# Stick-breaking attention, one core: the last pair of heads takes its query blocks in another order, and ScalarE's copies are reordered in every step

## The reference

```python
def block(args):                      # 128 queries, 16 heads of 64
    i, qi = args
    ...
    zlog = jnp.einsum('bqhd,bkhd->bhqk', qi, kp) * scale
    log_beta = jax.nn.log_sigmoid(zlog)
    log_keep = jnp.where(valid, log_beta - zlog, 0.0)
    after = lax.cumsum(log_keep, axis=3, reverse=True) - log_keep
    w = jnp.where(valid, jnp.exp(log_beta + after), 0.0)
    return jnp.einsum('bhqk,bkhd->bqhd', w, vp)
```

## Time and profile before

| | |
|---|---|
| median of 3 runs | 2334.75 us (2331.86 to 2334.78) |
| the profiled execution | 2333.68 us, its span 2331.9 us |
| TensorE busy in the span | 2202.1 us (94%) |
| VectorE busy | 1592.7 us (68%) |
| ScalarE busy | 1036.3 us (44%) |
| mean granted TensorE clock | 0.982 |

### The profile page before, as it was taken

How to read it: one execution, slowest core, us unless ns; L and a number is a source line. 1 busy time by engine, 2 the same in 40 slices (tenths; PEclk the granted TensorE clock), 3 DMA queues, 4 the chain that set the end, 5 groups by cost and what they waited for, 6 DMA issues and landing times. The chain is left out here.

```text
span 2331.9 us, 44629 instructions
## 1 busy us (share of the span) xinstructions
PE 2202.1 (94%) x18332; PEld 1411.5 (61%) x18332; DVE 1592.7 (68%) x2016; ACT 1036.3 (44%) x1883; POOL 607.0 (26%) x379
## 2 busy tenths in 40 slices
PE   7999998899999889989999999999999999999997
PEld 4666665555555556656666665458644445588846
DVE  7876887888888855787777774257688484236544
ACT  3226765667666643434444443235543232124221
POOL 3555762000000120064333331000256442001060
PEclk9999999999999989999999999999999999989998
DMA  3113213676766631211111113326333612032412
GB/s 130 48 52 101 82 55 71 116 130 125 135 126 126 110 107 63 94 41 50 55 55 59 55 51 118 101 74 212 124 102 104 212 55 82 23 101 72 158 60 73
DMA packets 279377, 216.24 MB, mean 93 GB/s; under 512 B 194752, under 2 KB 245120, under 8 KB 277776
## 3 DMA queue, kind: packets, MB, share of 16 engines
q1 hardware_dynamic: 279184, 213.51, 34.0%
HBM read 145.77 MB, written 25.76 MB: 74 GB/s over the span
## 5 line engine op out<-in xcount | busy, mean ns | idle before, releaser
L1519 DVE TENSOR_TENSOR_SCAN att_left<-att_left,att_unseen_prefix 16x16 f32<-16x16 f32 (+5 forms) x144 | 177.9, 1276 | 28.2 <-ACT att_left L1332 26.9
L2912 PE MATMUL ps<-second_x_hi,whi_z 128*128 128x512 f16 (+1 forms) x480 | 179.1, 373 | 2.6 <-DVE second_x_lo L1740 1.4
L1219 PE MATMUL ps<-x_hi,whi_z 128*128 128x348 f16 x560 | 176.7, 315 | 4.7 <-DVE att_q L1450 4.7
L2913 PE MATMUL ps<-second_x_lo,whi_z 128*128 128x512 f16 (+1 forms) x480 | 178.8, 372 | 0.0
L2914 PE MATMUL ps<-second_x_hi,wlo_z 128*128 128x512 f16 (+1 forms) x480 | 178.8, 372 | 0.0
L1221 PE MATMUL ps<-x_hi,wlo_z 128*128 128x348 f16 x560 | 175.3, 313 | 0.0
L1220 PE MATMUL ps<-x_lo,whi_z 128*128 128x348 f16 x560 | 175.3, 313 | 0.0
L1352 ACT ACTIVATE att_left_split<-att_left 128x256 f16<-128x256 f32 (+7 forms) x128 | 87.2, 681 | 111.9 <-DVE att_left L1519 111.1
L2215 PE MATMUL ps<-x_lo,whi_z 128*128 128x342 f16 x432 | 133.2, 308 | 0.0
L2214 PE MATMUL ps<-x_hi,whi_z 128*128 128x342 f16 x432 | 132.8, 308 | 0.0
L2216 PE MATMUL ps<-x_hi,wlo_z 128*128 128x342 f16 x432 | 132.6, 307 | 0.0
(11 more groups left out here) (657 smaller groups left out, 6438.7 us busy)
## 6 DMA issues: line engine op xcount, KB each, us to landing
wraw_z<-in_w_second SPq DMA_DIRECT2D x30, 512.0 KB, 3.6
wraw_z<-in_w_up SPq DMA_DIRECT2D x26, 512.0 KB, 3.5
wraw_z<-in_w_qkv SPq DMA_DIRECT2D x24, 512.0 KB, 4.2
wraw_z<-in_w_down SPq DMA_DIRECT2D x20, 512.0 KB, 4.3
raw_down<-in_w_down SPq DMA_DIRECT2D x20, 512.0 KB, 4.1
seg<-dt_a_sums SPq DMA_DIRECT2D x18, 512.0 KB, 5.1
wraw_z<-in_w_up SPq DMA_DIRECT2D x36, 256.0 KB, 3.7
second_work<-parked_units SPq DMA_DIRECT2D x7, 1280.0 KB, 6.0
```

The source lines that it names most:

```text
L1219: nc.tensor.matmul(lin_ps(g), hi, xhi, start=(kb == 0), stop=False)
L1519: nc.vector.tensor_tensor_scan(x, x, unseen, 1.0, ALU.mult, ALU.max).then_inc(s_scan, 1)
L2912: nc.tensor.matmul(out, hi, xhi, start=(j == 0), stop=False)
L2913: nc.tensor.matmul(out, hi, xlo, start=False, stop=False)
```

## The change

Three things change together. Pair 7 takes its blocks in the order 6, 7, 8, 3, 4, 5, 0, 1, 2; position in the pair is now `i`, and work that was bound to a pair's first steps (`v_steps`, `values_high`, `values_low`, `turn_v`, `copy_v`, `split_values`, the squares) goes by `i`, the lengths by `j`. The stash goes by `stash` (j = 3, or in pair 7 the first step), at the end of the two banks of each head. In every step ScalarE has `copy_w` and `split_high` ahead of `left_high(s, 1)` and `values_high`, and in the second step of a pair `copy_v` behind `left_high(s, 0)`. TensorE has `turn_v` in the middle of a projection and not ahead of it.

```diff
@@ -1020,10 +1020,26 @@
...
+LAST_ORDER = (6, 7, 8, 3, 4, 5, 0, 1, 2)
+SENDS = 2 * NSTEP - 1
+
+
+def sent_order(blocks):
+
+    counts = [2 * (j > 0) + (i == 0) for i, j in enumerate(blocks)]
+    return [sum(counts[:i]) for i in range(NSTEP)]
+
+
+SENT_OF = sent_order(range(NSTEP)), sent_order(LAST_ORDER)
+V_SENT = [SENDS * p + (2 if p == PAIRS - 1 else 0) for p in range(PAIRS)]
+
+
 class Step:
...
     def __init__(self, n):
-        self.n, self.p, self.j = n, n // NSTEP, n % NSTEP
+        self.n, self.p, self.i = n, n // NSTEP, n % NSTEP
+        self.j = self.i if self.p < PAIRS - 1 else LAST_ORDER[self.i]
+        self.stash = self.j == 3 if self.p < PAIRS - 1 else self.i == 0
         self.rows = P if self.j else META
@@ -1037,7 +1053,7 @@
...
-        return SENDS * self.p + 2 * self.j - 1 + a
+        return SENDS * self.p + SENT_OF[self.p == PAIRS - 1][self.i] + a
@@ -1055,7 +1071,6 @@
...
 PSCALE = 32768.0
-SENDS = 2 * NSTEP - 1
 SENT_SLOTS, SENT_SIGNALS = 3, 4
@@ -1106,7 +1121,7 @@
...
         z_ps = lambda a: flat[:, (2 + 2 * a) * BANK:(4 + 2 * a) * BANK]
-        z_more = flat[:, 2 * BANK:6 * BANK].rearrange("p (a n) -> p a n", a=2)[:, :, BANK:BANK + META]
+        z_more = flat[:, 2 * BANK:6 * BANK].rearrange("p (a n) -> p a n", a=2)[:, :, 2 * BANK - META:2 * BANK]
         turn_ps = S.ps[:, 6, :]
@@ -1147,7 +1162,7 @@
...
                 def turn_values(p):
-                    e = SENDS * p
+                    e = V_SENT[p]
                     sp.wait_ge(s_left_lo, e + 1)
@@ -1159,7 +1174,7 @@
...
                             turn_left(s, a)
-                    else:
+                    if ATT[s].i == 0:
                         turn_values(ATT[s].p)
@@ -1224,7 +1239,7 @@
...
                     t = ATT[n]
-                    if t.j == 0:
+                    if t.i == 0:
                         pe.wait_ge(s_low, 2 * NT * (t.p + 1))
@@ -1234,7 +1249,7 @@
...
                                                         start=(i == 0), stop=(i == 2))
-                    if t.j == 3:
+                    if t.stash:
                         for i, (x, y) in enumerate(PASSES):
@@ -1257,8 +1272,10 @@
...
                         pe.wait_ge(s_o, n)
-                    if t.j == 1:
-                        pe.wait_ge(*landed(SENDS * t.p))
+                    if t.i == 0:
+                        pe.wait_ge(s_vlo, t.p + 1)
+                    if t.i <= 1 and t.j:
+                        pe.wait_ge(*landed(V_SENT[t.p]))
                     if t.j:
@@ -1268,8 +1285,6 @@
...
                                                      skip_group_check=True)
-                    else:
-                        pe.wait_ge(s_vlo, t.p + 1)
                     pe.wait_ge(s_wlo, n + 1)
@@ -1285,10 +1300,12 @@
...
                         scores(s)
-                    if s < STEPS and ATT[s].j == 1:
+                    if s + GROUPS < (QKV_B + EARLY) * NT:
+                        linear(s + GROUPS, 0, DB // 2)
+                    if s < STEPS and ATT[s].i == 1:
                         turn_v(ATT[s].p)
                     if s + GROUPS < (QKV_B + EARLY) * NT:
-                        linear(s + GROUPS, 0, DB)
+                        linear(s + GROUPS, DB // 2, DB)
                     if 1 <= s <= STEPS:
@@ -1323,7 +1340,7 @@
...
                                 act.wait_ge(s_left_lo, ATT[n - 3].sent(1) + 1)
-                    if a == 1 and t.j == 3:
+                    if a == 1 and t.stash:
                         nc.scalar.activation(left_more[:, 0:META], z_more[:, 0, :], ACT.Sigmoid, scale=-0.125)
@@ -1417,27 +1434,26 @@
...
                             odds(s, a)
-                        if ATT[s].j == 1:
-                            copy_v(ATT[s].p)
                         if ATT[s].j:
                             left_high(s, 0)
+                        if ATT[s].i == 1:
+                            copy_v(ATT[s].p)
                     if s % NT == 0 and s // NT + BY_POOL < QKV_B + EARLY:
...
                         chunk_high(NORMED_AT[s - 1])
-                    if s < STEPS:
-                        if ATT[s].j:
-                            left_high(s, 1)
-                        else:
-                            values_high(ATT[s].p)
                     if 1 <= s <= STEPS:
...
                         split_high(s - 1)
+                    if s < STEPS and ATT[s].j:
+                        left_high(s, 1)
+                    if s < STEPS and ATT[s].i == 0:
+                        values_high(ATT[s].p)
                     if s >= LAG:
                         store(s - LAG)
-                    if s < STEPS and ATT[s].p and ATT[s].j == 4:
+                    if s < STEPS and ATT[s].p and ATT[s].i == 4:
                         square(ATT[s].p - 1)
@@ -1539,28 +1555,28 @@
...
                         continue
-                    if ATT[s].j == LAG:
+                    if ATT[s].i == LAG:
                         split_values(ATT[s].p)
...
                     scan(s, 1)
-                    if ATT[s].j == 0:
+                    if ATT[s].j:
+                        left_low(s, 0)
+                    if ATT[s].i == 0:
                         v_steps(ATT[s].p)
-                    else:
-                        left_low(s, 0)
                     if s + GROUPS in SPLIT:
...
                         left_low(s, 1)
-                    else:
+                    if ATT[s].i == 0:
                         values_low(ATT[s].p)
...
                     p = ATT[s].p - 1
-                    if p >= 1 and ATT[s].j == 5:
+                    if p >= 1 and ATT[s].i == 5:
                         add_square(p)
...
```

## The result

The changed kernel takes 2342.81 us (median of 7 runs, 2340.23 to 2345.68) against 2333.86 for the kernel before (7 runs, 2329.51 to 2334.78): ratio 1.0040, interval 1.0028 to 1.0052. It is slower, by 9 us where +1.5 was forecast. The profiled execution took 2341.88 us, 8.2 more than that of before.

What follows compares the result with a forecast made beforehand. TensorE was taken as the bound (94% busy), with VectorE close behind. Pair 7's order -7.4, copies +5.4 and clock +3.5 gave +1.5 us on the profiled 2333.7, so 2335.2, stated as 2336; range 2326 to 2344.

Steps and rivals of the forecast that it cites:

- the likeliest case: Whole kernel: shorter tail paid back by VectorE's lag and boundary waits; 2336 us, within 0.2%, chance 0.40.
- The copies, +1.1 a pair: Pairs 2 to 6: copies moved in every step make VectorE late; TensorE waits 1.3 and 2.5; +5.4 us in all.
- Two more stretches of half clock, +3.5: Pair boundaries: longer waits drop TensorE's clock to 1.2 GHz twice more, +3.5 us, between none and six (10.5).
- Rival B: Pair boundaries: the longer wait drops the clock at every one, 1.75 us each; all six give 2343 us; chance 0.31.
- Pair 7's order, -7.4: Pair 7 and tail: the new order shortens the tail by 12.6 us and costs 5.2 inside the pair.
- 3.0 was reckoned for the long values: Inside pair 7: 18 long value blocks move ahead out of the tail, about 0.17 us each at full clock.
- 2.2 was reckoned: Inside pair 7: new waits of 7.8 us against 5.6 of waits before, so +2.2 us.
- the forecast 7.8: Pair 7: two new TensorE waits, 2.7 us for v_steps before turn_v and 5.1 for copy_v.
- the 2.2 of the kernel before's "long blocks": Pair 7: 2.2 us of earlier waits in its long blocks, counted among the 5.6 set against the new waits.
- not 7.1: Tail: from the end of the last projection to the next phase 7.1 us, 12.6 less than 19.74.
- the 0 for pairs 0 and 1: Pairs 0 and 1: later low parts still end with GpSimd's work, so 0 us; shared bandwidth instead would cost 4.5 more.

Runs made afterwards that it cites:

- e3: The changed kernel with copy_v back ahead of left_high(s, 0): 2332.55 us, ratio 0.9997 to the kernel before.
- e7: The kernel before with copy_w and split_high ahead of left_high(s, 1) at j = 3 and 6 alone: 2349.47 us, ratio 1.0066 to the kernel before.
- e9: The changed kernel with GpSimd's two output-weight conversions on 16 of 1024 columns (wrong weights, timing only): 2336.39 us, ratio 1.0016 to the kernel before.
- e10: The changed kernel with copy_v ahead of left_high(s, 0), copy_w and split_high ahead only in a pair's first step and j = 7, 8: 2321.57 us, ratio 0.9950.
- e1: The changed kernel with pair 7 in natural order, the copies as changed: 2341.27 us, ratio 1.0033 to the kernel before.

## Where the prediction held and where it failed, point by point

The range held the time (2326 to 2344); the likeliest case and the centre missed it. That the range reached so far was in part luck: its upper end was put there for the clock falling at all six boundaries, which did not happen. By the prediction's own steps:

- **The copies, +1.1 a pair, nothing in pairs 0 and 1, 5.4 in all.** Right in size. Pair 3 pays 1.06. Pair 2 begins 0.06 earlier than before, so pairs 0 and 1 cost nothing in sum; but that is a net figure, as TensorE's idle time in them rose by 0.5 and its busy time fell by 0.6, with 3.4 us less at half clock in pair 0. The waits are 1.16 (forecast 1.3) and 2.38 (forecast 2.5). The copies alone are 7.9 slower, where this term and the next make 8.9. The prediction gave VectorE's lag as the cause and `copy_v` as the place where it shows; e3 has the same lag (1.17 before the meta product in pair 3, as the changed kernel has in pair 4) and pays nothing in pairs 2 to 6, so in this kernel the cost needs `copy_v`'s place as well.
- **Two more stretches of half clock, +3.5.** Right in size at the boundaries: pairs 2 and 5 have one each at about 1.6. Both terms together, 8.9, are what pair 7's start is late, 8.8. Rival B's drop at all six boundaries did not come: its time was reached in another way.
- **Pair 7's order, -7.4: the step that failed.** The profiles give 75.37 to 74.08, -1.3, and the missing 6.1 falls into three pieces. *TensorE's busy time inside the pair* rose by 5.8 (50.03 to 55.80), where 3.0 was reckoned for the long values. The rest is half clock inside pair 7: 6.8 us at 0.52 that begin inside the wait of 4.89, and 3.4 at 0.53 behind the wait of 2.38, some 4.3 us lost where the earlier trace rows's stretch lost 1.7, so 2.6 more. The clock term spoke of boundaries alone. *Its waits* rose by 4.4 (5.60 to 9.96), where 2.2 was reckoned. 2.56 and 4.89 are 7.45, the forecast 7.8. The prediction let the 2.2 of the kernel before's "long blocks" go; but 1.5 of those stood behind the same collision of GpSimd and VectorE, which with the new order falls on the j = 5 block again and costs 2.38 (the two rows of the kernel before below). *The tail* is 8.3 and not 7.1: its low part takes 1.98 in place of 0.40, which with the rest as reckoned would give 8.7. With short GpSimd work the tail is about 6.8 (822.8 to 829.57). 2.6 + 2.2 + 1.2 make 6.0 of the 6.1.

```profile
790.30 4.26 DVE L1478 SCALAR_TENSOR_TENSOR att_left_split<-att_left,att_left_split 128x640 f16<-128x640 f32 x2
```

```profile
796.91 0.23 PE L1274 MATMUL ps<-att_w_meta_split,att_v_meta_split 96*128 96x128 f16 x1 [1.51 <-DVE att_w_meta_split L1462]
```

- **The two parts do not add.** The order alone gained 3.7 us, the change lost 9.0. The prediction summed the terms as if the copies in pair 7 were free. In the tail they put VectorE's low part behind GpSimd's start: the tail is 8.3 with both, 6.4 with the order alone, and about 6.8 with both and short GpSimd work. Of the 4.3 us between the two pairs 7 that is 1.9; the other 2.4 lies for the most part in the steps of its second and third block (15.9 and 7.5 us against 14.3 and 6.5). It was not taken apart.
- **Outside the attention** 0.7 of the 8.2 remains: the stage begins 0.75 earlier in the profile after and what follows its end takes 1.4 longer, with the first 5.08 us of the next phase at 0.50. The prediction put this at nothing; in the other profiles what follows the end of the attention varies from 1500.8 to 1506.2 us (before: 1503.2), so no effect of the change is shown there.
- **VectorE beside GpSimd.** The reading of the earlier trace rows fits what followed, but the 0 for pairs 0 and 1 does not prove it: e7, with copies ahead at j = 3 and 6, paid 1.8 in them. It should have been looked for in pair 7 and the tail, where the same trace had it. The Trainium skill, "SBUF — State Buffer", section "SBUF: two separate sides", says that whichever of the two starts first keeps the shared ports for its whole instruction. The runs agree: with GpSimd's work in quarters VectorE's step took 5.25 in place of 7.8. The reverse is there too: in e9 GpSimd's high part of 16 columns, begun at 808.13 beside a scan of VectorE, takes 1.29 and ends with the scan at 809.42, where 0.20 is enough at 823.16 with VectorE idle.
- **What stays open.** Why the half clock falls after some boundary waits of 2.4 and not after others: the trace shows it behind two of the seven. Why e7 pays 1.7 a pair where the changed kernel pays 1.1 for slips at the same two steps: that the boundary copies give part back is argued above and was not run. What `turn_v` in the middle of the projection is worth by itself is open too.
- **A row that misleads.** The wait of 4.89 is put down to a DMA. With short GpSimd work (e9) the profile puts the same wait, again 4.89, down to `copy_v`, and moving `copy_v` forward (e3) took it to 1.0: `copy_v` it was.

## What to carry to other kernels

An operation moved ahead in an engine's queue is free only in the steps where that engine stands waiting at this point, so decide it step by step and not for the whole loop: with copies ahead in every step the kernel was 11.0 us slower than with copies ahead in a pair's first step and at j = 7 and 8 alone (e3 against e10). Move each operation by itself as well: `copy_v`, which went along, cost 10.3. A shorter tail has to be paid from inside; before reckoning it, list what the other engines run in the stretch to which the work moves, GpSimd above all. Where two changes touch the same steps, measure each alone: here one gained 3.7, the other lost 7.9, and both together lost 9.0.

## What the runs showed of the hardware that was not expected

Beside GpSimd's instructions of 1024 columns two scans of VectorE took 5.56 instead of 2.94 us and two low parts 4.26 instead of about 1.6. Cut into four, GpSimd's three operations take 3.91, 4.62 and 3.44 us (1.04, 3.21 and 2.25 whole), and the kernel is no slower for it (3.2 us faster by medians). Seven waits of up to 2.4 us in the same code dropped the granted clock twice, and in e1 too it fell behind two boundaries, but behind others (pairs 2 and 6, not 2 and 5), so a term for the clock is best given as a count with both ends.
